# Three additions of the gated-linear-attention block moved from VectorE to GpSimd

## The reference, cut to what matters

```python
bc = jnp.cumsum(to_chunks(log_a), axis=-2)
...
def step(S, inp):
    q_c, k_c, v_c, b_c = inp
    o_inter = jnp.einsum('bhcd,bhde->bhce', q_c * jnp.exp(b_c), S)
    diff = b_c[:, :, :, None, :] - b_c[:, :, None, :, :]
    dmat = jnp.exp(jnp.where(mask, diff, -jnp.inf))
    scores = jnp.einsum('bhid,bhjd,bhijd->bhij', q_c, k_c, dmat)
    o_intra = jnp.einsum('bhij,bhje->bhie', scores, v_c)
    b_last = b_c[:, :, -1:, :]
    S = (S * jnp.exp(b_last[:, :, 0, :])[..., None]
         + jnp.einsum('bhcd,bhce->bhde', k_c * jnp.exp(b_last - b_c), v_c))
    return S, o_inter + o_intra
...
o_f = gla_chunked(q_h, k_h, v_h, heads(log_a[:, :, 0], GLA_DK))
o_b = flip(gla_chunked(flip(q_h), flip(k_h), flip(v_h), flip(heads(log_a[:, :, 1], GLA_DK))))
```

## Time and profile before

| | |
|---|---|
| median of three runs | 3192.82 us (3191.23 to 3199.42) |
| the profiled execution | 3199.42 us, of which the span is 3197.6 us |
| TensorE, VectorE, ScalarE, GpSimd busy | 2947.9, 1462.3, 1158.9, 278.6 us |
| mean granted clock of TensorE | 0.951 of full speed |
| `gla_mix` | from about 244 to 378 us of the span |

### The profile page before, as it was taken

One profiled execution on the slowest core, in us unless ns is written; L12 is line 12 of the kernel. 1 busy time (PEld: TensorE's weight loads), 2 busy tenths in 40 slices (PEclk: granted clock), 3 DMA queues, 4 the chain that ended last, 5 costly groups with the idle time before them and its releaser, 6 DMA issues.

```text
span 3197.6 us, 57141 instructions
## 1 busy us (share of the span) xinstructions
PE 2947.9 (92%) x25280; PEld 2414.6 (76%) x25280; DVE 1462.3 (46%) x2041; ACT 1158.9 (36%) x1896; POOL 278.6 (9%) x318
## 2 busy tenths in 40 slices
PE   6966699788888699999999999999999999999997
PEld 5845577578877287888888887787887888888886
DVE  4638754234444444533244324766445533234323
ACT  4655365222221334322232324533234333242322
POOL 1000022344442200000000000000000000000000
PEclk8976799979999699999999999999999999999998
DMA  3410053311100032222222222222222222223222
GB/s 129 134 52 5 9 186 135 100 44 34 44 14 4 28 138 86 92 93 99 97 92 95 93 99 99 86 90 89 99 95 90 93 93 98 96 96 124 94 99 79
DMA packets 99160, 273.37 MB, mean 85 GB/s; under 512 B 8161, under 2 KB 35297, under 8 KB 98785
## 3 DMA queue, kind: packets, MB, share of 16 engines
q1 hardware_dynamic: 90128, 237.19, 21.7%
q0 software_dynamic: 8784, 32.51, 3.0%
HBM read 257.09 MB, written 12.58 MB: 84 GB/s over the span
## 4 chain that ended last, share of the span: by engine, by line
PE 61%; DVE 2%; ACT 1%; issue 0%; DMA 0%; DVEq 0%; ACTq 0%
PE be_ps L2761 45%; PE be_ps L2782 15%; DVE be_ring L2551 1%; PE be_ps L2795 1%; PE be_ps L2503 0%; PE be_ps L2497 0%; ACT be_whi L2828 0%; DVE be_raw_r L2934 0%; DMA be_raw<-in_ple_gate 0%; DVE be_total L2516 0%; DVE ext_r L2561 0%; DVE big L2524 0%; ACT big L2834 0%; DVE big L2533 0%; ACT be_ring L2458 0%
## 5 line engine op out<-in xcount | busy, mean ns | idle before, releaser
L2934 DVE TENSOR_TENSOR be_raw_r<-be_raw,be_whi 128x1024 fp32r<-128x1024 f32 x361 | 442.2, 1225 | 985.1 <-ACT be_whi L2828 984.9
L2761 PE MATMUL be_ps<-ext_r,be_whi 128*128 128x512 f32 x2304 | 713.9, 391 | 15.2 <-PEq L2171 8.6
L2828 ACT CAST be_whi<-be_raw 128x1024 fp32r<-128x1024 f32 x361 | 378.7, 1049 | 856.5 <-DMA be_raw<-in_ffn_down 314.8
L2761 PE MATMUL be_ps<-big_r,be_whi 128*128 128x512 f32 x2048 | 643.1, 395 | 2.4 <-DVE big_r L2559 2.4
L2761 PEld LDWEIGHTS be_ps<-ext_r,be_whi 128*128 128x128 f32 x2304 | 432.6, 188 | 107.9 <-issue 10.2
L2761 PEld LDWEIGHTS be_ps<-big_r,be_whi 128*128 128x128 f32 x2048 | 384.0, 188 | 97.3 <-DVE big_r L2559 2.8
L2761 PE MATMUL be_ps<-ext_r,be_raw_r 128*128 128x512 f32 x1152 | 449.5, 390 | 0.0
L2761 PE MATMUL be_ps<-big_r,be_raw_r 128*128 128x512 f32 x1024 | 408.4, 399 | 0.0
L2782 PE MATMUL be_ps<-ext_r,be_whi 128*128 128x512 f32 x1152 | 354.9, 389 | 0.0
L2761 PEld LDWEIGHTS be_ps<-ext_r,be_raw_r 128*128 128x128 f32 x1152 | 217.1, 188 | 45.6
L2782 PEld LDWEIGHTS be_ps<-ext_r,be_whi 128*128 128x128 f32 x1152 | 216.2, 188 | 45.1
(11 more groups left out here) (324 smaller groups left out, 3888.2 us busy)
## 6 DMA issues: line engine op xcount, KB each, us to landing
be_raw<-in_ffn_gate SPq DMA_DIRECT2D x88, 512.0 KB, 3.2
be_raw<-in_ffn_up SPq DMA_DIRECT2D x88, 512.0 KB, 3.2
be_raw<-in_ffn_down SPq DMA_DIRECT2D x88, 512.0 KB, 3.2
be_raw<-in_conv_in SPq DMA_DIRECT2D x48, 512.0 KB, 3.2
gp_ada<-in_ada POOLq DMA_DIRECT2D x24, 512.0 KB, 3.5
rp_ada<-in_ada POOLq DMA_DIRECT2D x24, 512.0 KB, 3.7
rwkv_prepared<-big SPq DMA_DIRECT2D x16, 512.0 KB, 3.5
be_raw<-in_w_out SPq DMA_DIRECT2D x16, 512.0 KB, 3.2
```

What stands on the lines that cost most here:

```text
L2761: mm = pe.matmul(ps[:, bank], part[:, k * P:(k + 1) * P], xs(k), start=(k == 0 and i == 0), stop=(k == KD - 1 and i == 2))
L2828: act.copy(w.hi[:, n % 3], w.raw[:, n % 3]).then_inc(w.hi_ready, 1)
L2934: dve.tensor_tensor(w.lo(n), w.raw[:, n % 3], w.hi[:, n % 3].bitcast(F32), ALU.subtract).then_inc(w.lo_ready, 1)
```

## The change

The three additions behind the masking product leave VectorE's program and become GpSimd's program in this stage, with marks of their own (`pool_made`). GpSimd's first addition waits for the product's mark `masked`. TensorE's `add_low_scores` and the next block's masking product, which overwrites `gm_part`, wait for GpSimd's `low`. Nothing else moves, and the arithmetic is the same.

```diff
-            dve_steps += {4: ["state"], 6: ["masked", "sum3", "sum1", "low"]}.get(n, [])
+            dve_steps += {4: ["state"], 6: ["masked"]}.get(n, [])
...
+        pool_made = Marks(core.sem("gm_pool"), ["sum3", "sum1", "low"])
...
+        @block.gpsimd
+        def _(pool):
+            pool_made.begin(pool)
+            for j in range(NBLK):
+                pool.wait_ge(*dve_made.by("masked", j))
+                pool.tensor_tensor(part[:, :, 0:3], part[:, :, 0:3], part[:, :, 3:6], ALU.add).then_inc(*pool_made("sum3"))
+                pool.wait_ge(*pool_made.by("sum3", j))
+                pool.tensor_tensor(part[:, :, 0], part[:, :, 0], part[:, :, 1], ALU.add).then_inc(*pool_made("sum1"))
+                pool.wait_ge(*pool_made.by("sum1", j))
+                if j >= 2:
+                    pool.wait_ge(*pe_out.by("low", j - 2))
+                pool.tensor_tensor(low[:, j % 2], part[:, :, 0], part[:, :, 2], ALU.add).then_inc(*pool_made("low"))
...
             def add_low_scores(j):
 
-                pe.wait_ge(*dve_made.by("low", j))
+                pe.wait_ge(*pool_made.by("low", j))
...
                 if j:
-                    dve.wait_ge(*dve_made.by("low", j - 1))
+                    dve.wait_ge(*pool_made.by("low", j - 1))
                 dve.tensor_tensor(part.rearrange("p a n t -> p a (n t)"), ps_low[:, :, 0:n_low * 2 * sub],
                                   mask[:, :].rearrange("p (a t) -> p a t", a=1).to_broadcast([P, 2, n_low * 2 * sub]),
                                   ALU.mult).then_inc(*dve_made("masked"))
-                dve.wait_ge(*dve_made.by("masked", j))
-                dve.tensor_tensor(part[:, :, 0:3], part[:, :, 0:3], part[:, :, 3:6], ALU.add).then_inc(*dve_made("sum3"))
-                dve.wait_ge(*dve_made.by("sum3", j))
-                dve.tensor_tensor(part[:, :, 0], part[:, :, 0], part[:, :, 1], ALU.add).then_inc(*dve_made("sum1"))
-                dve.wait_ge(*dve_made.by("sum1", j))
-                if j >= 2:
-                    dve.wait_ge(*pe_out.by("low", j - 2))
-                dve.tensor_tensor(low[:, j % 2], part[:, :, 0], part[:, :, 2], ALU.add).then_inc(*dve_made("low"))
```

## The result

The changed kernel takes 3227.05 us (median, 3225.89 to 3228.23) against 3195.02 us before, in alternating runs: ratio 1.0100, 95% interval 1.0083 to 1.0117. That is +32.0 us, 1.0% slower. The forecast was 3193.3 us with 3185 to 3210 us as its range, and 0.78 on no change. The rival that was called "GpSimd is starved" had 3222 us and 0.17 (with its partial forms).

A forecast was written before the change was run, and what follows sets the result against it. TensorE bounds the kernel (92% busy), but in this stage a dependence loop with VectorE busiest does. Seven boundaries' -0.35 us plus +0.8 us at the end gave +0.45 us: 3193.3 us against the median, range 3185 to 3210 us.

The forecast's parts named there:

- GpSimd is starved: Rival: VectorE's row keeps the port until L1030's wait; +4.1 us a block, +29.5 us, 3222 us; chance 0.17 wholly or partly.
- The shared resource: Gated-linear-attention stage: two-SBUF-input VectorE instructions and SBUF-reading GpSimd ones exclude each other; the moved 1.84 us runs between VectorE's pieces.
- the gap between streams: VectorE's 0.27 us streams repeat every 0.34 us, taken as leaving a gap in which GpSimd gets its turn.
- the slack of 1.5 us: How much later the low-score sum may come before ScalarE's copy of the high scores moves; about 1.5 us.
- the copy: ScalarE's copy of the high scores, at 342.97 in the traced block; a shift of it shifts the block.
- The ceiling: Most that removing three VectorE additions could gain: 1.34 us per block boundary, at most 9.4 us over seven.
- GpSimd's prices: Estimated undisturbed GpSimd additions: 0.98 us for 128x384, 0.43 us for each 128x128, 1.84 us in all.
- the exclusion in both directions: VectorE and GpSimd block each other: the later instruction waits for the earlier one's end, adding the overlap less 0.12 to 0.14 us.
- The sum of a block: Step times from L1010 to the second L1019 with alternating turns: -0.05 us per block boundary, -0.35 us over seven.
- The end of the stage: Last block, where nothing covers the sum: GpSimd's three free-running additions end at 373.56 instead of 372.77, +0.8 us.

The follow-up runs named there:

- e1_own_waits: The changed kernel with four waits of VectorE for its own last instruction added behind the masking product; 3199.48 us, ratio 1.0011 to the kernel before.
- g3_one_wait: The changed kernel with a single wait of VectorE for its own last instruction, behind a block's first pair of differences; 3196.69 us, ratio 1.0009 to the kernel before.
- g1_reader_across: The changed kernel with a spare 128x384 GpSimd addition per block, reaching from the masking product into VectorE's row; 3198.32 us, ratio 1.0006 to the kernel before.

## Why the prediction was wrong

**The step that failed** is in "The shared resource": that VectorE "gets one instruction in while GpSimd goes from one to the next", taken from the gap between streams of 0.27 us repeated every 0.34 us, with only the end of a single blocking instruction as evidence. That row says nothing on a row of such instructions: behind the L1351 that held GpSimd's L1411 comes L1328, which reads PSUM. In the changed kernel the gap lets nobody in: seven times out of seven GpSimd waited through 13 instructions, and its 128x384 addition took 5.93 us where the sum had 1.10 us (339.49 to 340.59). The sum was then beyond the slack of 1.5 us, and the copy 4.4 us late. The wait runs show that a single break ends the hold, and the fills that it is one of reading.

**The ceiling** of 1.34 us for a block was right: 1.32 us in the run whose fills don't contend. The block of 16.8 us was one of the longer ones; the mean is 16.24 us. No term of the sum hangs on it.

**GpSimd's prices** were right: 0.99, 0.45 and 0.45 us against 0.98, 0.43 and 0.43; and so was the exclusion in both directions, to 0.01 us in the cases worked out above.

**The sum of a block** with alternating turns, -0.05 us, was near for kernels in which turns do alternate: 0.00, +0.01 and +0.14 us in e1_own_waits, g3_one_wait and g1_reader_across, each of which has a wait or a spare addition besides. What the sum didn't say is that the changed kernel isn't such a kernel.

**The end of the stage**: +0.8 us forecast, +0.9 us measured.

**The starved rival** had the place and the order right: VectorE's stop before L1030 of level 1 (forecast 5.17 us behind the masking product's end, 344.58 less 339.41; measured 5.15 us, 346.93 less 341.78), GpSimd's last sum 6.99 us behind it (measured 7.06 us), +4.1 us for a block (4.42 us) and +29.5 us in all (+32.0 us). It was short by 0.3 us for a block: the copy stood at 7.84 us and not at 7.66 us, and in most blocks before at 3.46 us, not at the 3.56 us of the earlier trace rows. It got 0.17 because two mechanisms were weighed by a gap in a record and not by a case of it; the rows had no case, and so gave no reason for odds far from one half.

**Not settled**: what in the chip keeps the port with VectorE over a row; whether turns alternate because a GpSimd reader reaches into the row or because GpSimd's next addition follows directly on it; and how long after a reader's end the alternation still begins (0.12 us of overlap did it, 0.24 to 0.31 us of distance didn't). Distances between weren't tried.

## What to carry to other kernels

Before an addition goes from VectorE to GpSimd, look at what VectorE does in the microseconds behind its release: in a row of instructions with two SBUF inputs and no break, a GpSimd instruction that reads SBUF may come last, not next. Put it under instructions that read PSUM, or give VectorE one short wait, which here brought the time back to before's but no gain; and compare the whole delay with the slack of whoever needs the result. A gain computed from "the engine is idle" stands on that slack.

## What was not expected of the hardware

- A GpSimd addition of two SBUF tensors (0.99 us) was held for 4.9 us by 13 successive VectorE instructions, though a single such instruction with none behind it let GpSimd in at its end (L1411 in the earlier trace rows).
- A break of 0.03 or 0.04 us in the records of VectorE ends the hold, and from there turns alternate without breaks (1.44, 0.52, 0.52 us).
- Where a GpSimd reader still runs for 0.12 to 0.13 us into the row's first instruction and GpSimd's next addition follows within 0.08 us, turns alternate too, though that instruction isn't stretched.
- A fill on GpSimd (0.42 us for 128x384) isn't held at the same place.
